# Summing three of five conditioning rounds on VectorE, with TensorE adding only over the partitions

## What is computed

```python
mod = silu(c) @ ada_w[layer] + ada_b[layer]      # 1024 -> 6 * 1024, once for the latent stream (c)
                                                 # and once for the context stream (c_ctx)
h = modulate(rmsnorm(x, norm_g), shift, scale)
pl = h @ ab_w_in                                 # layer 0: 1024 -> 3072: q, k, v, gate, LRU u, LRU y
rc, rl = retention_bidir(...)                    # from q, k, v
lc, ll = rglru_bidir(conv(u), gate_w, ...)       # 8 units: 2 directions x 4 channel tiles
x = x + gate * (concat([ret, rec]) @ ab_w_out)   # then a mixture of experts, then layer 1 the same way
```

## Time and profile before

| what | value |
|---|---|
| median of 3 runs | 2066.79 us (2065.3 to 2068.74) |
| the profiled execution | 2067.23 us, span 2065.6 us |
| mean granted TensorE clock | 0.916 of full speed |
| PE busy, whole span | 1719.8 us (83%) |
| DVE, ACT, POOL busy, whole span | 679.7, 438.4, 272.5 us |
| first matmul of the 40 groups, last end | 40.14 us, 354.74 us |
| DMA, whole span | 559.64 MB, mean 271 GB/s |

### The profile page before, as it was taken

The page is one execution under the profiler, slowest core; times in us unless marked ns, Lnnn a source line. Parts: engine busy times, 40 slices in busy tenths (PEclk is TensorE's granted clock), DMA queues, the critical chain, the costliest instruction groups (busy, mean ns, idle before and its releaser), DMA issues. The chain is left out here.

```text
span 2065.6 us, 26627 instructions
## 1 busy us (share of the span) xinstructions
PE 1719.8 (83%) x9184; PEld 874.9 (42%) x9185; DVE 679.7 (33%) x1211; ACT 438.4 (21%) x842; POOL 272.5 (13%) x393
## 2 busy tenths in 40 slices
PE   5999999899799799997538999999978899765561
PEld 3443344745344334443216445555534344333230
DVE  3403775643311111111124437775431111111115
ACT  3104443211001100111114125553101101101102
POOL 1002450311101100101013230000121000000001
PEclk9999999999899899999878999999979899878775
DMA  9877744530789999999962202001459999999994
GB/s 372 276 266 254 247 165 143 192 114 31 306 321 403 415 418 409 419 412 410 423 267 88 86 1 92 1 1 54 174 229 398 414 409 415 418 415 421 420 388 152
DMA packets 99608, 559.64 MB, mean 271 GB/s; under 512 B 17188, under 2 KB 37376, under 8 KB 59976
## 3 DMA queue, kind: packets, MB, share of 16 engines
q1 hardware_dynamic: 87152, 524.49, 63.9%
q0 software_dynamic: 7744, 20.98, 2.9%
q10 hardware_dynamic: 4632, 13.11, 1.7%
HBM read 522.88 MB, written 40.91 MB: 273 GB/s over the span
## 5 line engine op out<-in xcount | busy, mean ns | idle before, releaser
L2176 PE MATMUL exp_gps<-moew_wg,all_hT 128*64 128x512 f32 (+1 forms) x480 | 247.8, 642 | 45.9 <-DMA moew_wu<-in_moe_w_up 40.2
L2170 PE MATMUL exp_gps<-moew_wg,all_hT 128*32 128x256 f32 x1088 | 162.7, 466 | 134.4 <-DMA moew_wu<-in_moe_w_up 127.0
L2177 PE MATMUL exp_ups<-moew_wu,all_hT 128*64 128x512 f32 (+1 forms) x480 | 246.7, 639 | 0.0
L588 PE MATMUL abp_ps<-ab_w,all_hT 128*128 128x512 f32 x384 | 169.8, 597 | 0.6 <-PE abp_ps L588 0.3
L2170 PE MATMUL exp_ups<-moew_wu,all_hT 128*32 128x256 f32 x1088 | 162.4, 465 | 0.0
L2170 PEld LDWEIGHTS exp_gps<-moew_wg,all_hT 128*32 128x32 f32 x1088 | 72.7, 133 | 205.5 <-issue 178.6
L2176 PEld LDWEIGHTS exp_gps<-moew_wg,all_hT 128*64 128x64 f32 (+1 forms) x480 | 79.4, 171 | 175.2 <-issue 174.2
L2325 DVE TENSOR_TENSOR all_hT<-all_hT,exp_ups 64x512 f32<-64x512 f32 (+1 forms) x30 | 20.7, 690 | 366.1 <-ACT all_hT L2261 366.1
L2217 PE MATMUL exp_yps<-moew_wd,all_hT 128*64 128x512 f32 (+1 forms) x240 | 115.1, 596 | 0.2 <-issue 0.2
L2219 PE MATMUL exp_yps<-moew_wd,all_hT 128*64 128x512 f32 (+1 forms) x240 | 115.1, 596 | 0.0
L588 PEld LDWEIGHTS abp_ps<-ab_w,all_hT 128*128 128x128 f32 x384 | 71.4, 190 | 99.1 <-issue 97.5
(11 more groups left out here) (428 smaller groups left out, 2566.4 us busy)
## 6 DMA issues: line engine op xcount, KB each, us to landing
moew_wg<-in_moe_w_gate SPq DMA_DIRECT2D x64, 2048.0 KB, 27.7
moew_wu<-in_moe_w_up SPq DMA_DIRECT2D x64, 2048.0 KB, 34.1
moew_wd<-in_moe_w_down SPq DMA_DIRECT2D x64, 2048.0 KB, 35.3
all_X<-in_ada_w SPq DMA_DIRECT2D x40, 1024.0 KB, 8.4
ys<-abp_zero SPq DMA_DIRECT2D x32, 448.0 KB, 8.8
ab_w<-in_ab_w_in SPq DMA_DIRECT2D x6, 2048.0 KB, 9.2
ab_rows<-in_ada_w SPq DMA_DIRECT2D x6, 1024.0 KB, 15.4
ys<-abp_zero SPq DMA_DIRECT2D x11, 512.0 KB, 6.8
```

Of the source, the lines that this page charges most:

```text
L588: last = nc.tensor.matmul(ps[i % RB][:], hT[:, kk, what * P:(what + 1) * P], w[n % S][:, kk, :], start=(kk == 0), stop=(kk == KD - 1))
L2170: last = nc.tensor.matmul(bank[lo + j * Q:lo + (j + 1) * Q, 0:HC], x[:, k, 0:Q], wt[:, k, j * HC:(j + 1) * HC], start=(k == 0), stop=(k == ...
L2176: nc.tensor.matmul(gps[0:rows, :], x[:, k, 0:rows], w.g[q][:, k, :], start=(k == 0), stop=(k == KD - 1))
L2177: last = nc.tensor.matmul(ups[at:at + rows, :], x[:, k, 0:rows], w.u[q][:, k, :], start=(k == 0), stop=(k == KD - 1))
```

## The change

Rounds 2 and 3 stay as they were, eight steps on PE each, one after every group (groups 2 to 9 and 26 to 33), over a ring of two buffers. Rounds 1, 4 and 5 go to DVE: for each chunk and stream `total = chunk * s[:, kk] + total`, where `s[:, kk]` is one number per partition, so that after eight chunks `total` (128 by 2048) holds per partition what is left to be added over the partitions. PE does this in `reduce` with a stationary operand of zeros and one column of ones (`pick`). Round 1 has both streams, rounds 4 and 5 the latent one alone. The chunks have a ring of four buffers of their own. DVE's order is: chunks 0 and 1, then 2 and 3 inside the tables, 4 to 7 one after each convolution tile, then 8 to 23 without anything between but two `ada_out`; unit 0 comes behind them. On SP the loads and stores of zeros are reordered to fit: 32 of 40 paired stores are issued by group 19.

```diff
-        RING = 3
+        TURNED = (2, 3)
+        SUMMED = (1, 4, 5)
+        ORDER = (2, 1, 4, 5, 3)
...
+        x_parts = [c.X[:, 2 * i:2 * i + 2, :].rearrange("p t n -> p (t n)") for i in range(3)]
+        row_parts = [flat_rows[:, i * AC:(i + 1) * AC] for i in range(6)]
+        ada_ring = x_parts[0:2]
+        RING = len(ada_ring)
+        sum_ring = [row_parts[0:3] + x_parts[2:], x_parts[0:2] + [row_parts[2]] + x_parts[2:]]
+        SR = len(sum_ring[0])
+        sums = {1: row_parts[3:5], 4: row_parts[5:6], 5: row_parts[3:4]}
...
-        ADA_AT = [2 + 7 * r + r // 4 + at for r in range(ROUNDS - 1) for at in (0, 1, 1, 2, 2, 3, 3, 4)]
+        ADA_AT = [2 + n for n in range(KD)] + [26 + n for n in range(KD)]
+        SUM_AT = [2, 3, 5, 6, 8, 9, 11, 12] + [12 + n // 2 for n in range(KD)] + [16 + n // 2 for n in range(KD)]
+        REDUCE_AT = {15: 1, 18: 4, 21: 5}
+        OUT_AT = {9: 0, 16: 1, 19: 2, 23: 3, 33: 4}
...
             sp.wait_ge(scaled, NT)
-            for n in range(RING):
-                ring_chunk(n)
+            sp.wait_ge(first_used, 3)
+            for n in range(SR):
+                if n < RING:
+                    ring_chunk(n)
+                sum_chunk(n)
...
                 for n in range(len(ADA_AT)):
                     if ADA_AT[n] == i:
-                        if n + RING < len(ADA_AT):
+                        if n + RING < KD:
+                            sp.wait_ge(ring_used, n + 1)
+                            ring_chunk(n + RING)
+                        elif KD <= n and n + RING < len(ADA_AT):
                             sp.wait_ge(ring_used, n + 1)
                             ring_chunk(n + RING)
                         clear_slots(n)
...
+                for n in range(len(SUM_AT)):
+                    if SUM_AT[n] == i:
+                        if n == KD - SR:
+                            sp.wait_ge(ring_used, KD)
+                        sp.wait_ge(sum_used, n + 1)
+                        sum_chunk(n + SR)
+                        clear_slots(len(ADA_AT) + n)
+                        if n + 1 == len(SUM_AT):
+                            for m in range(RING):
+                                ring_chunk(KD + m)
+                if i in OUT_AT:
+                    n = OUT_AT[i]
+                    l, cols = ada_columns(ORDER[n])
+                    sp.wait_ge(mod_done, n + 1)
+                    for st in range(2):
+                        sp.dma_start(c.mods[st, l, cols].rearrange("(j n) -> j n", n=512),
+                                     bias_rows(bias, st)).then_inc(stored, 16)
+                    sp.wait_ge(stored, 32 * (n + 1))
+                    if n + 1 < len(ORDER):
+                        load_bias(sp, ORDER[n + 1], bias, b_ready)
...
+            def reduce(r):
+                n = SUMMED.index(r)
+                pe.wait_ge(sum_used, KD * (n + 1))
+                pe.wait_ge(mod_done, ORDER.index(r))
+                if n == 0:
+                    pe.wait_ge(picked, 2)
+                for st, total in enumerate(sums[r]):
+                    for j in range(4):
+                        last = nc.tensor.matmul(aps[32 * j:32 * j + 32, :], pick[:, st, :], total[:, j * 512:(j + 1) * 512],
+                                                start=(st == 0), stop=(st + 1 == len(sums[r])))
+                last.then_inc(reduced, 1)
...
+            def ada_sum(n):
+                r, kk = SUMMED[n // KD], n % KD
+                buf = sum_ring[n >= KD][n % SR]
+                dve.wait_ge(sum_ready[n % SR], 16 * (n // SR + 1))
+                if n:
+                    dve.wait_ge(sum_used, n)
+                if n == 2 * KD:
+                    dve.wait_ge(reduced, 1)
+                for st, total in enumerate(sums[r]):
+                    s_col = sT[:, kk, st:st + 1]
+                    if kk == 0:
+                        last = V.tensor_scalar(total, buf, s_col, None, ALU.mult)
+                    else:
+                        last = V.scalar_tensor_tensor(out=total, in0=buf, scalar=s_col, in1=total, op0=ALU.mult, op1=ALU.add)
+                last.then_inc(sum_used, 1)
...
             for ct in range(LT):
-                if ct == LT - 1:
-                    ada_out(1)
...
+                ada_sum(LT + ct)
+                if ct == 2:
+                    ada_out(2)
+            for n in range(KD, 2 * KD):
+                ada_sum(n)
+            ada_out(1)
+            for n in range(2 * KD, 3 * KD):
+                ada_sum(n)
+            ada_out(4)
+            out_before = {2: 5, 7: 3}
```

More of the change, by code:

```diff
@@ L396, in ab_project @@
         ring_ready = [s.sem(f"ring_ready{i}") for i in range(RING)]
+        sum_ready = [s.sem(f"sum_ready{i}") for i in range(SR)]
+        sum_used, reduced, picked = s.sem("sum_used"), s.sem("reduced"), s.sem("picked")
         (w_free, mm, ev_act, cleared, z_set, z_stored, p_ready, gw_ready, x_ready, gates, sig,
@@ L492, in _ @@
                         clear_slots(n)
[L493 to L503, removed]
+                for n in range(len(SUM_AT)):
[18 more added lines that the diff above has]
+                        load_bias(sp, ORDER[n + 1], bias, b_ready)
+            for b in range(len(ADA_AT) + len(SUM_AT), BLOCKS):
                 clear_slots(b)
@@ L512, in _ @@
             nc.gpsimd.memset(bias[:], 0.0).then_inc(zeroed, 1)
+            nc.gpsimd.memset(pick[:], 0.0).then_inc(zeroed, 1)
+            pool.wait_ge(zeroed, 4)
+            for st in range(2):
+                nc.gpsimd.memset(pick[:, st, st:st + 1], 1.0).then_inc(picked, 1)
             tables.early(pool)
@@ L626, in _ @@
             act.dma_start(laid[NB:NL, :], a["lru_lambda"][0].rearrange("d (c p) -> (d c) p", p=P)).then_inc(p_ready, 16)
-            act.wait_ge(zeroed, 3)
+            act.wait_ge(zeroed, 4)
             load_bias(act, 0, bias0, b0_ready)
-            load_bias(act, 1, bias, b_ready)
+            load_bias(act, ORDER[0], bias, b_ready)
             act.wait_ge(c_ready, 32)
@@ L699, in _ @@
             W = U_LEN - PADL - PADR
-            def ada_out(r):
-                dve.wait_ge(b_ready, 32 * r)
-                dve.wait_ge(ring_used, KD * r)
+            def ada_sum(n):
[13 more added lines that the diff above has]
+                last.then_inc(sum_used, 1)
+            def ada_out(r):
+                n = ORDER.index(r)
+                dve.wait_ge(b_ready, 32 * (n + 1))
+                if r in TURNED:
+                    dve.wait_ge(ring_used, KD * (TURNED.index(r) + 1))
+                else:
+                    dve.wait_ge(reduced, SUMMED.index(r) + 1)
                 V.tensor_add(bias[:], aps[:], bias[:]).then_inc(mod_done, 1)
@@ L746, in _, with between @@
                                     ALU.mult, ALU.add).then_inc(aff_dve, 1)
-            tables.vector(dve)
+            def between(part):
+                for n in range(2 * part, 2 * part + 2):
+                    ada_sum(n)
+            tables.vector(dve, between)
             V.tensor_scalar(n4[:], k.sp[:, 2 * RH:], LRU_C / 2, None, ALU.mult).then_inc(n4_done, 1)
@@ L833, in gpsimd, with vector @@
                                     pattern=[[0, RH], [sign, P]], channel_multiplier=-sign).then_inc(masked, 1)
-    def vector(dve):
+    def vector(dve, between):
         link = Chain(dve, chain)
@@ L845, in vector @@
         dve.wait_ge(e_in, 1)
+        between(0)
         dve.wait_ge(e_out, 1)
@@ L863, in vector @@
         V.tensor_scalar(k.dec[:], lg3, float(P), None, ALU.mult).then_inc(dcols, 1)
+        between(1)
         dve.wait_ge(masked, 2)
```

13 lines of the change are left out of this document (9 added, 4 removed).

## The result

| | before | after |
|---|---|---|
| median, the same chips side by side | 2068.23 us (7 runs) | 2056.08 us (7 runs) |
| ratio, with its 95% interval | | 0.9937 (0.9923 to 0.9951) |
| the profiled execution's span | 2065.6 us | 2054.4 us |
| mean granted TensorE clock | 0.916 | 0.908 |
| PE, DVE, ACT, POOL busy | 1719.8, 679.7, 438.4, 272.5 | 1706.9, 753.9, 437.9, 286.2 |

One of the seven executions of the kernel after took 2562.14 us at a granted clock of 0.656; the ratio is taken without it, and without it the median is 2055.8. The kernel is faster by 0.6%, some 13 us (10 to 16 by the interval). The forecast was 2065 us in a range of 2055 to 2075: the time lies in the range, at its lower edge, and what happened is the first rival, "the chunks come sooner", not the case that I held for likeliest.

The account below looks back on a forecast made before the run. PE's work list was taken to bound the first stage. Its terms, -17.9 - 7.0 + 7.5 + 15.8 = -1.6 us on the median 2066.79, gave 2065 us, range 2055 to 2075.

Parts of the forecast that it names:

- the first rival: DMA queue: pairs take 3.7 us, last chunk at 184 to 187; about -5.5 to -8.5 us, at most 2049; 34%.
- the case that I held for likeliest: Whole kernel: the forecast of 2065 us, within 0.2% of the old time, 2062.7 to 2070.9; 39%.
- far end: First stage: sums done by 180, unit 0 delays nothing; stage 17.4 us shorter, 2049 us.
- the price of a pair: DMA queue: a chunk and a store of zeros, 1.507 MB, take 3.85 us; 15 pairs from chunk 8 take 57.8.
- the idle queue behind a store: DMA at the stores of rounds 2 and 1: SP stands, 4.6 us idle each time, 9.2 for two.
- part 3: DMA queue: round 2's chunks come late on PE, +7.5 us; the sums' last chunk comes at 190.5.
- Part 5: PE before groups 22 and 24: waits for late unit 0, with slower clock; +15.8 us, 12.5 of it before group 22.
- Part 3's waits of round 2: PE behind groups 6 and 9: chunks 1.3 and 3.5 us late, plus 2.8 of slower clock; +7.5 us.
- Part 2: PE, first stage: two old chunk waits of 4.2 us and 2.8 us of slower clock go; -7.0 us.
- Part 1: PE, first stage: ada steps of 37.75 us become 16 single steps and reductions, 19.85; -17.9 us.
- Part 4: DVE: 2.35 us a multiply-add, 71 us in all, hidden under DMA; POOL's slowing at most 4 us.
- The rule against the change: DMA: HBM side binds at about 358 GB/s a core, so a pair would take 4.2 us all along.

Follow-up runs that it names:

- zeros later: Changed kernel with the 24 stores of zeros that went with the sums' chunks issued behind groups 20 to 23; 2041.0 us, again 2039.06 us.
- both: Changed kernel with 24 stores of zeros behind groups 20 to 23 and SP's wait for a stored round two groups later; 2037.7 us, again 2038.49 us.
- half of the zeros: Changed kernel with 12 of the 24 stores of zeros beside the sums' chunks issued behind groups 20 to 23; 2047.4 us.
- split wait: Changed kernel with SP waiting for a stored round and loading the next bias row two groups later, issuing chunks in between; 2050.13 us.
- more for DVE: Changed kernel with 1.05 us more DVE work for each of chunks 8 to 23; 2058.34 us.
- eleven stores more: Changed kernel with 11 later stores of zeros issued with the sums' chunks, beside the 24 there; 2069.74 us.
- the kernel before with late zeros: Kernel before with its first 16 stores of zeros issued at the end of the stage, 2067.53 us; spread beside steps 16 to 31 instead, 2061.32 us.
- the kernel with fewer steps: Kernel before without the matmuls of rounds 1, 4 and 5, loads kept; 2118.45 us, unusable as a total; first stage ends 23.28 us sooner.

## Why the prediction was right and wrong

All kernels with the sums, by when unit 0 started:

| kernel | unit 0 | stage end | difference |
|---|---|---|---|
| zeros later (twice), both (twice) | 165.1 to 168.8 | 328.0 to 329.2 | |
| half of the zeros | 178.34 | 337.29 | 158.9 |
| split wait | 182.28 | 341.06 | 158.8 |
| after (twice) | 187.98, 188.51 | 345.40, 345.92 | 157.4 |
| more for DVE | 190.86 | 348.28 | 157.4 |
| eleven stores more | 199.56 | 356.97 | 157.4 |

From 178 us on the stage ends some 158 us behind unit 0's start, whatever the cause of its lateness. The prediction had 193.5 and 353.1, so 159.6, one for one: the right place, the right engines, the right law. The two differences of 159 belong together: from unit 0's start to group 22 it was 12.1 us with half of the zeros and 12.0 with the split wait (10.6 in the four others), because POOL ran beside unit 0's first instructions there.

Where the line ends depends on when PE gets to group 22. With the zeros later it was there at 184.4, so with a way of 12.1 us unit 0 has to start by 172; the prediction said 180 or 181, for a PE that came later, since it had round 2's waits ahead of it and less relief. Its far end, 2049 us, still had these waits in it (7.5). 2041 us was to be had because moving the zeros took them away as well, and because PE was relieved of some 1.8 us more than I had counted (-26.7 in all, where parts 1 and 2 gave -24.9).

**Step that failed: the price of a pair, and of the idle queue behind a store (part 3).** It gave the last chunk at 190.5; it came at 185.6. Chunk 9, at 122.2 by the sum (117, a pair, and the 1.3 of a second store of zeros), came at 121.4, 0.7 sooner. From there to chunk 23 there are 14 pairs; at 3.62 instead of 3.85 they are 3.2 us shorter. The two stores cost 2.8 and 3.5 us of the row instead of 4.6 each, 3.0 less; the weight block 5.4 as counted (5.2). Against that chunk 15 came 5.1 us behind chunk 14, 1.5 more than a pair (so too in the second execution); nothing on record says why. The rest, 0.4 us, is in small pieces. So the pair was the largest of the terms that were mis-sized, and the idle queue behind the two stores the second, nearly as large, and both pointed one way. Both numbers of the pair stood in the rows: 3.7 us between two landings, and 392 GB/s, which I took as the steady rate. With 15 pairs in a row behind one another a difference of 0.2 us a pair was enough to part the forecast from the first rival. Unit 0, at 193.5 by the sum, came at 188.51.

**Part 5, +15.8 said, 13.7 measured.** Waits 1.17 and 9.31 (said 12.5), clock 2.1 (1.9), group 24 1.1 (1.4). Besides unit 0 being 5.0 sooner, the way from its start to group 22 was 199.12 - 188.51 = 10.6 us (said 12.3). The prediction took 10.8 us to the square root from unit 0 before; there POOL was at work beside it, and an instruction of 0.56 us took 2.05. After, POOL had its part done. POOL and DVE in the kernel before, and the same instruction of DVE in the one after:

```profile
188.44 2.38 POOL L523 TENSOR_TENSOR abp_gt<-abp_gt,ab_yT 128x768 f32<-128x768 f32 x1
189.20 2.05 DVE L775 TENSOR_SCALAR abp_xc<-abp_ri 128x768 f32<-128x768 f32 x1
```

```profile
196.07 0.56 DVE L858 TENSOR_SCALAR abp_xc<-abp_ri 128x768 f32<-128x768 f32 x1
```

Against that PE itself was 4.7 us earlier at the place than said, and only waited longer for it.

**Part 3's waits of round 2, +7.5 said (its three terms, 1.3, 3.5 and 2.8, give 7.6), 5.3 measured.** 0.22 + 2.55 + 0.91 us of waiting, and the clock fell once, behind the longest wait: 0.75 for the step and 0.8 for the group, where 2.8 was said. The order of the two was the other way round: the step behind group 6 waited longer (said 1.3), that behind group 9 shorter (said 3.5). In the second execution, on another chip, it was 4.2 us of waiting and no fall of the clock. The 2.8 were taken from a wait of 3.3 us, and a wait of 2.55 has the fall in one execution and not in the other.

**Part 2, -7.0 said, -7.4** by the kernel before with late zeros.

**Part 1, -17.9 said, -20.4 left over** when the other terms, as measured, are taken from -8.8 (-8.8 + 7.4 - 5.3 - 13.7). The reductions cost what was said (139.88 to 141.73 is 1.85, 164.02 to 165.01 is 0.99). Of the 2.5 us more, 24 times 0.06 to 0.08 = 1.4 to 1.9 are what the kernel with fewer steps shows: groups that follow one another with no step between take 6.93 us (20.80 for three, 141.73 to 162.53), one between steps 7.06. Another 0.9 lies in the first three groups, 15.37 us here, 16.27 before; among all kernels run they take 15.4 to 16.9, so that is scatter. The terms close to within 0.3 us. None of it was worth anything as long as unit 0 was late.

**Part 4 was right**: 2.35 and 1.29 us, hidden. POOL did slow two sums (3.31 and 2.52 us), within the bound, and they delayed nothing. Its count of POOL's work was short, though: before 190 us there is also the stretch from 183 on, the one that the earlier trace rows has in it.

**The rule against the change.** The windows between 130 and 170 us had 410 GB/s. The Trainium skill ("DMA: Bandwidth & Descriptors", section "Where 436 GB/s comes from") has the HBM side binding at about 358 GB/s a core. These runs don't agree: with the pauses taken out (split wait), 35 us stretches run at 396 and 398. It could have been read before the forecast, too. The prediction says of 400 GB/s or more that "no long stretch but the first" has it, but the profile of the whole execution has longer ones behind the first stage. The window over the experts of layer 0 in the kernel before, nearly all loads of 2 MB, with small stores:

```profile
620.00:1035.00 415.00, 361.30 (x2139) 170.35 (x2141) 65.47 (x119) 46.68 (x92) 33.70 (x75) 0.94 1.01 414
```

At 414 GB/s a pair takes 3.64 us, which is what it took. The mixture of loads and stores is another there, so the row decides nothing alone; but it speaks for the first rival, and neither the steady rate nor the chances took account of it.

Why the stretch of 115 to 135 us before had only 357 at a busy share of 1.00 wasn't tried; what differs is that two or three transfers were in its queue, where more were now.

**The chances.** The case that I gave 39% failed by two things that pointed one way: unit 0 came 5.0 us sooner, and the way from it to the stage's end was 2.2 us shorter (157.4, not 159.6). Its sum for the stage was too high by these 7.2 us. The first rival had given -5.5 for pairs of 3.7 us with the clock falling in round 2, which it did; -8.8 came. The other 2.4 us are scatter that the range had to hold as well.

## What to carry to other kernels

When work moves to an engine that takes its data as it lands, price the landing of the last byte, with everything that the queue carries between: here 0.45 MB of zeros beside each 1 MB chunk cost 0.85 us each of the start of the unit that all waited for, and moving them was worth as much as the change itself or more (15 us against 12 to 13). Before taking a rate as the steady one, look for the longest stretch in the whole trace where the queue is full. A wait for a small store on the engine that issues the loads drains the queue behind it (6.3 us for two); put the wait behind later issues. And before delaying any work to the end of a stage, see which engine then reaches the barrier last.

## What was unexpected about the hardware

- One queue with loads of 1 MB and stores of 0.45 MB by turns ran at 410 GB/s over 40 us (396 and 398 over 35 us each with the store of a round in it), as fast as the loads of the experts (414) and faster than any 20 us stretch of the first stage before but its opening (417). Landings of a chunk took up to 15.6 us meanwhile, without a loss of rate.
- POOL and DVE side by side slow one another, and not always both. A POOL multiply of 0.83 us (at 179.41, with DVE idle) took 2.87 at 171.09, and the sum beside it (170.92) kept its 2.35 us. The sum that took 3.31 us (174.69) ran beside POOL's product at 175.93, and that one was slowed as well: 3.39 us, where the same line took 1.47 at 210.14. Rows of POOL:

```profile
171.09 2.87 POOL L563 TENSOR_SCALAR abp_gt<-abp_gt 128x768 f32<-128x768 f32 x1 [23.72 <-ACT abp_gt L742]
...
175.93 3.39 POOL L559 TENSOR_TENSOR abp_gt<-ab_yT 128x768 f32<-128x768 f32 x1
179.41 0.83 POOL L560 TENSOR_SCALAR abp_gt<-abp_gt 128x768 f32<-128x768 f32 x1
```

- Leaving a step out from between two groups on PE gives back more than the step: 1.00 to 1.02 us instead of 0.94 on the average of 24.
